# Modulation sums interleaved with the next group's products, and the last pair's normalisation moved into the output projection

## The reference, cut to what matters

```python
mod_lat = jax.nn.silu(c) @ w_mod[l] + b_mod[l]          # 9 x 1024 values, and the same for c_ctx
...
h = _modulate(_rmsnorm(x, norm_g[0]), sh1, sc1)
x = x + 0.5 * g1[:, None, :] * _swiglu(h, ffn_gate[0], ffn_up[0], ffn_down[0])
...
y_sum = ys[0] + ys[1]
mean = jnp.mean(y_sum, axis=-1, keepdims=True)          # over the 64 values of a head
var = jnp.mean(jnp.square(y_sum - mean), axis=-1, keepdims=True)
y_gn = ((y_sum - mean) * lax.rsqrt(var + GN_EPS)).reshape(B, S, D_RWKV) * ln_w + ln_b
gate = jax.nn.sigmoid(gd) @ g2
y_rwkv = (y_gn + (bonuses[0] + bonuses[1]).reshape(B, S, D_RWKV)) * gate
mixed = jnp.concatenate([y_four, y_rwkv], axis=-1).astype(h.dtype)
return mixed @ w_out, finals[0], finals[1]
```

## Time and profile before

| | |
|---|---|
| median of 3 runs | 2886.95 us (2882.22 to 2894.52) |
| the profiled execution | 2874.92 us |
| its span in the trace | 2873.1 us |
| PE busy | 2657.5 us (92%) |
| DVE busy | 1440.4 us (50%) |
| ACT busy | 702.7 us (24%) |
| mean granted TensorE clock | 0.949 of full speed |

### The profile page before, as it was taken

One profiled execution on the slowest core, in us unless ns is written; L12 is line 12 of the kernel. 1 busy time (PEld: TensorE's weight loads), 2 busy tenths in 40 slices (PEclk: granted clock), 3 DMA queues, 4 the chain that ended last, 5 costly groups with the idle time before them and its releaser, 6 DMA issues. The chain is left out here.

```text
span 2873.1 us, 51540 instructions
## 1 busy us (share of the span) xinstructions
PE 2657.5 (92%) x21182; PEld 2522.9 (88%) x21182; DVE 1440.4 (50%) x2749; ACT 702.7 (24%) x1340; POOL 87.7 (3%) x158
## 2 busy tenths in 40 slices
PE   5999999999999799976979797869999999999998
PEld 3999999999999799945868676669999999999998
DVE  4654455555533866317484867433733333433444
ACT  3311111111112411124444454221411111111113
POOL 0000000000000000000111120200000000000000
PEclk8999999999999899987898898989999999999999
DMA  7222222222210222242121212050211111111101
GB/s 277 66 81 75 82 68 80 70 82 82 82 37 1 61 78 93 71 182 53 43 64 40 64 40 64 12 184 27 76 41 41 44 44 44 31 42 44 44 22 67
DMA packets 216144, 193.84 MB, mean 67 GB/s; under 512 B 64787, under 2 KB 184382, under 8 KB 215998
## 3 DMA queue, kind: packets, MB, share of 16 engines
q1 hardware_dynamic: 206512, 166.49, 18.4%
q10 hardware_dynamic: 9486, 25.26, 3.2%
HBM read 159.01 MB, written 32.70 MB: 67 GB/s over the span
## 5 line engine op out<-in xcount | busy, mean ns | idle before, releaser
L129 PE MATMUL ff_ps<-h_hi,ff_wlo 128*128 128x384 f32 x2112 | 712.3, 337 | 7.3 <-DVE h_lo L478 3.7
L131 PE MATMUL ff_ps<-h_hi,ff_whi 128*128 128x384 f32 x2112 | 710.1, 336 | 0.0
L130 PE MATMUL ff_ps<-h_lo,ff_whi 128*128 128x384 f32 x2112 | 709.7, 336 | 0.0
L674 DVE TENSOR_TENSOR ff_s<-ff_ps,ff_s 128x384 f32<-128x384 f32 x132 | 73.6, 557 | 680.6 <-PE ff_ps L131 678.3
L129 PEld LDWEIGHTS ff_ps<-h_hi,ff_wlo 128*128 128x128 f32 x2112 | 400.0, 189 | 10.9 <-DVE h_lo L478 6.7
L130 PEld LDWEIGHTS ff_ps<-h_lo,ff_whi 128*128 128x128 f32 x2112 | 400.3, 190 | 0.0
L131 PEld LDWEIGHTS ff_ps<-h_hi,ff_whi 128*128 128x128 f32 x2112 | 399.6, 189 | 0.0
L129 PE MATMUL ff_ps<-ff_uhi,ff_wlo 128*128 128x384 f32 x1056 | 355.6, 337 | 10.9 <-DVE x L685 10.9
L131 PE MATMUL ff_ps<-ff_uhi,ff_whi 128*128 128x384 f32 x1056 | 353.0, 334 | 0.0
L130 PE MATMUL ff_ps<-ff_ulo,ff_whi 128*128 128x384 f32 x1056 | 352.9, 334 | 0.0
L613 ACT ACTIVATE ff_s<-ff_ps 128x384 f32<-128x384 f32 x132 | 64.9, 491 | 775.8 <-PE ff_ps L131 775.8
(11 more groups left out here) (289 smaller groups left out, 3300.9 us busy)
## 6 DMA issues: line engine op xcount, KB each, us to landing
ff_n<-w_mod ACTq DMA_DIRECT2D x64, 384.0 KB, 3.3
ff_raw<-ffn_w_gate SPq DMA_DIRECT2D x44, 512.0 KB, 4.0
ff_raw<-ffn_w_up SPq DMA_DIRECT2D x44, 512.0 KB, 4.0
ff_raw<-ffn_w_down SPq DMA_DIRECT2D x44, 512.0 KB, 4.5
md_w<-w_mod SPq DMA_DIRECT2D x3, 4096.0 KB, 30.6
pj_raw<-w_in SPq DMA_DIRECT2D x19, 512.0 KB, 4.0
z_dram<-pj_zo SPq DMA_DIRECT2D x15, 576.0 KB, 2.9
rw_rkv<-z_dram SPq DMA_DIRECT2D x12, 576.0 KB, 5.8
```

Source lines behind the costliest of these rows:

```text
L129: pe.matmul(out, w_lo, x_hi, start=start, stop=False)
L130: pe.matmul(out, w_hi, x_lo, start=False, stop=False)
L131: return pe.matmul(out, w_hi, x_hi, start=False, stop=stop)
L674: dve.tensor_tensor(hid[:, t % 2, :], ps[:, 2 + t % 2, 0:CW], silu[:, t % 2, :], ALU.mult)\
```

## The change

Three things are edited.

1. `Modulation.sum` no longer stands at a group's end. Its 12 matmuls are issued one by one in the next group, each behind one k step (three matmuls) of the first gate tile (8 of them) and the first up tile (4). `keep` moves behind the next group's first hidden tile on DVE. Groups 1 and 9 are written out beside the loop.
2. The two slices behind updates 11 and 19 on DVE are each parted by vector: one instruction behind updates 9, 11, 17 and 19.
3. `rw_last` is gone. Its work stands in `output_stage`, among the loads and splits of that stage, and the last row of the mixed input is taken from SBUF (`y`) instead of being stored to DRAM and loaded. Buffers of the RWKV stage that it needs are kept in SBUF until the end of the output stage.

```diff
-        if k:
+        if k or not isinstance(g, int):
             act.wait_ge(self.used, g * (2 * KD) + (2 * k - 2 * KD))
         else:
-            act.wait_ge(self.kept, g)
+            act.wait_ge(self.kept, 1)
...
+    def slice(self, dve, g, k, vectors=(0, 1)):
+        for s in vectors:
+            if s == vectors[0]:
+                dve.wait_ge(self.w_in, g * (16 * KD) + (16 * (k + 1) - 16 * KD))
+                if k:
+                    dve.wait_ge(self.used, g * (2 * KD) + (2 * k - 2 * KD))
...
-    def sum(self, pe, g):
-        pe.wait_ge(self.used, g * (2 * KD))
-        pe.wait_ge(self.kept, g)
-        for j in range(self.COLS // P):
-            for s in range(2):
-                last = pe.matmul(self.ps[:, 2 * j + s:2 * j + s + 1], self.acc[:, s, j * P:(j + 1) * P],
-                                 self.sb["cst"][:, C_ONE:C_ONE + 1], start=True, stop=True)
-        last.then_inc(self.summed, 1)
+    def sum(self, pe, g, n):
+
+        if n >= 2 * self.COLS // P:
+            return
+        if n == 0:
+            pe.wait_ge(self.used, g * (2 * KD) - 2 * KD)
+            pe.wait_ge(self.kept, g - 1)
+        j, s = divmod(n, 2)
+        ins = pe.matmul(self.ps[:, n:n + 1], self.acc[:, s, j * P:(j + 1) * P], self.sb["cst"][:, C_ONE:C_ONE + 1],
+                        start=True, stop=True)
+        if n == 2 * self.COLS // P - 1:
+            ins.then_inc(self.summed, 1)
 
     def keep(self, dve, g):
-        dve.wait_ge(self.summed, g)
+        dve.wait_ge(self.summed, g - 1)
...
+                                if rest and t == 0:
+                                    rest.sum(pe, g, base // 2 * KD + k)
...
                 group(0, True)
                 if rest:
-                    with pe.Fori(1, rest.BLOCKS + 1) as g:
+                    group(1, False)
+                    with pe.Fori(2, rest.BLOCKS + 1) as g:
+                        group(g, False, rest=rest)
+                    group(rest.BLOCKS + 1, False, rest=rest)
+                else:
+                    with pe.Fori(1, GROUPS - 1) as g:
                         group(g, False)
-                        rest.sum(pe, g)
-                with pe.Fori(1 if rest is None else rest.BLOCKS + 1, GROUPS - 1) as g:
-                    group(g, False)
                 group(GROUPS - 1, False, True)
...
-                def group(g, last=False, opening=False, rest=None):
+                def group(g, last=False, opening=False, rest=None, keep=None):
                     for t in range(NC if opening else 0, TILES):
                         hidden(g, t)
+                        if keep and t == 0:
+                            keep.keep(dve, g)
                         if rest:
                             rest.slice(dve, g, t)
...
-                        if n in (11, 19) and rest:
-                            rest.slice(dve, g, TILES + (n == 19))
+                        if n in (9, 11, 17, 19) and rest:
+                            rest.slice(dve, g, TILES + (n > 15), (n // 2 % 2, ))
...
-                    with dve.Fori(1, rest.BLOCKS + 1) as g:
-                        group(g, rest=rest)
-                        rest.keep(dve, g)
+                    group(1, rest=rest)
+                    with dve.Fori(2, rest.BLOCKS + 1) as g:
+                        group(g, rest=rest, keep=rest)
+                    group(rest.BLOCKS + 1, keep=rest)
...
+def output_stage(nc, io, sb, rw, md, xd):
...
+        act_t = Steps(st.sem("act_s"), ["w0", "sq", "w1", "gate", "m0", "sqrt", "m1", "m2", "m3", "m4", "affine", "m5", "m6", "m7"] +
+                      [f"w{o}" for o in range(2, KD)])
+        dve_t = Steps(st.sem("dve_s"), ["y", "centre", "w0", "w1", "var", "m0", "inv", "wide", "m1", "m2", "norm0", "norm1", "m3",
+                                        "norm2", "m4", "bonus", "m5", "gate", "m6", "m7"] +
                       [n for o in range(KD) for n in [f"x{o}_{c}" for c in range(NC)] + [f"w{o + 2}"] * (o + 2 < KD)])
...
-                for k in range(KD):
+                for k in range(LAST):
...
                 upper(0)
+                dve_t.wait(act, "centre")
+                act_t.did("sq", act.activation(c2, y, ACT.Square))
                 upper(1)
-                for k in range(KD):
-                    act.wait_ge(m_in[k % MS], 16 * (k // MS + 1))
-                    act_t.did(f"m{k}", act.activation(m_hi[:, k, :], m[:, k % MS, :], ACT.Copy))
+                pe_t.wait(act, "gate")
+                act_t.did("gate", act.activation(b3(gate), ps[:, 3:6, 0:CW], ACT.Copy))
+                row(0)
+                dve_t.wait(act, "var")
+                act_t.did("sqrt", act.activation(inv, inv, ACT.Sqrt))
+                for k in range(1, 5):
+                    row(k)
+                dve_t.wait(act, "norm2")
+                act_t.did("affine", act.activation(y, y, ACT.Identity, bias=par("ln_b"), scale=par("ln_w")))
+                for k in range(5, KD):
+                    row(k)
                 for o in range(2, KD):
                     upper(o)
...
+                dve_t.wait(pe, "y")
+                over("mean", 0, sb["cst"][:, C_BLK:C_BLK + P], y)
+                over("gate", 3, rw.g2[:, :], rw.lora[:, 2, :])
+                act_t.wait(pe, "sq")
+                pe_t.did("var", head_sums(pe, sb, ps[:, VAR, :], c2))
+                row(0)
+                dve_t.wait(pe, "wide")
+                for c in range(2):
+                    pe_t.did(f"root{c}", spread(pe, sb, ps[:, ROOT[c], :], wide, c))
+                row(1)
+                dve_t.wait(pe, "norm0")
+                pe_t.did("root2", spread(pe, sb, ps[:, ROOT[2], :], wide, 2))
+                for k in range(2, KD):
+                    row(k)
...
+                def norm(c):
+                    pe_t.wait(dve, f"root{c}")
+                    dve_t.did(f"norm{c}", dve.tensor_tensor(y[:, cols3(c)], ps[:, ROOT[c], 0:CW], y[:, cols3(c)], ALU.mult))
+                dve_t.did("y", dve.tensor_tensor(y, y, yb, ALU.add))
+                pe_t.wait(dve, "mean")
+                dve_t.did("centre", dve.scalar_tensor_tensor(b3(y), ps[:, 0:3, 0:CW], -1.0 / HS, b3(y), ALU.mult, ALU.add))
                 lower(0)
                 lower(1)
-                for k in range(KD):
-                    act_t.wait(dve, f"m{k}")
-                    dve_t.did(f"m{k}", dve.tensor_tensor(m_lo[:, k, :], m[:, k % MS, :], m_hi[:, k, :].bitcast(F32), ALU.subtract))
+                pe_t.wait(dve, "var")
+                dve_t.did("var", dve.tensor_scalar(inv, ps[:, VAR, 0:2 * NT], 1.0 / HS, GN_EPS, ALU.mult, ALU.add))
+                row(0)
+                act_t.wait(dve, "sqrt")
+                dve_t.did("inv", dve.reciprocal(inv, inv))
+                dve_t.wait(dve, "inv")
+                dve_t.did("wide", widen(dve, wide, inv))
+                row(1)
+                row(2)
+                norm(0)
+                norm(1)
+                row(3)
+                norm(2)
+                row(4)
+                act_t.wait(dve, "affine")
+                dve_t.did("bonus", dve.tensor_tensor(y, y, rw.bonus[:, :], ALU.add))
+                row(5)
+                act_t.wait(dve, "gate")
+                dve_t.wait(dve, "bonus")
+                dve_t.did("gate", dve.tensor_tensor(y, gate, y, ALU.mult))
+                row(6)
+                row(7)
...
-def rw_last(nc, sb, rw, md, p):
...
-        rw_last(nc, sb, rw, md, NP - 1)
+    return rw
```

More of the change, by code:

```diff
@@ L555, in _, with group @@
             def _(pe):
-                def group(g, first, last_one=False):
+                def group(g, first, last_one=False, rest=None):
                     if first:
@@ L649, in _ @@
                 if rest:
-                    with act.Fori(1, rest.BLOCKS + 1) as g:
+                    group(1, rest=rest)
+                    with act.Fori(2, rest.BLOCKS + 1) as g:
                         group(g, rest=rest)
@@ L1041, in _ @@
                     act_t.did(f"S{j}", act.activation(sine[:, j, :], ps[:, 4 + j, :], ACT.Copy))
-def output_stage(nc, io, sb, md, xd):
-    RAW, MS = 2, 4
-    x = sb["x"]
+def output_stage(nc, io, sb, rw, md, xd):
+    RAW, MS, LAST = 2, 4, KD - 1
+    x, y, yb, wide, c2 = sb["x"], rw.y[:, :], rw.work[:, 2 * T:3 * T], rw.work[:, 0:T], rw.work[:, T:2 * T]
+    gate = rw.work[:, 3 * T:4 * T]
+    b3 = lambda t: t.rearrange("p (c n) -> p c n", c=NC)
+    cols3 = lambda c: slice(c * CW, (c + 1) * CW)
+    inv = rw.mp[:, 0, 0:2 * NT]
+    par = lambda n: rw.pp[:, PP[n]:PP[n] + 1]
     with Stage(nc) as st, nc.psum_tensor("op_ps", [P, 8, 512], F32) as ps, \
@@ L1085, in upper, with row @@
                     act_t.did(f"w{o}", act.activation(w_hi[:, o % 2, :], raw[:, o % 2, :], ACT.Copy))
+                def row(k):
+                    if k < LAST:
+                        act.wait_ge(m_in[k % MS], 16 * (k // MS + 1))
+                    else:
+                        dve_t.wait(act, "gate")
```

(32 more changed lines are left out.)

103 lines of the change are left out of this document (22 added, 81 removed).

## The result

| | before | changed |
|---|---|---|
| first timing: median (lowest to highest, runs) | 2884.59 (2879.56 to 2894.52, 4) | 2842.47 (2836.92 to 2844.58, 4) |
| second timing | 2879.94 (2871.18 to 2889.66, 11) | 2850.08 (2844.31 to 2856.73, 6) |
| profiled execution, span | 2873.1 | 2835.1 |

The ratio is 0.9847 (0.9816 to 0.9878) in the first timing and 0.9888 (0.9866 to 0.9909) in the second. I had 2854 us and a ratio of 0.9886. Faster, as forecast, but by 42 us in the first timing where I had 33; its median lies 11.5 us under my 2854, at the very low end of my range. The second timing, by 30 us, fits.

What follows compares the result with a forecast made beforehand. PE, busy for 92% of the span, was taken as the bound. The terms 0 - 9.5 - 3.4 - 20.1 = -33.0 us, taken from the median 2886.95, gave 2854 us (chance 0.69); range 2842 to 2870 us.

Steps and rivals of the forecast that it cites:

- A1, the pair's price: Modulation's sums on PE, spread as 12 pairs a group: 0.224 us a pair, 2.69 us a group as before, so 0 us.
- R1: Rival, chance 0.11: each pair of spread sums costs a drain, 0.36 us instead of 0.224; +13 us, 2867 us.
- A1, the clock: PE's clock behind the modulation's sums no longer drops once they are spread: six drops of 1.59 us, -9.5 us.
- R2: Rival, chance 0.05: the clock does not hold through the interleaved stretch in groups 2 to 9; 9.2 us a group, 2937 us.
- A2: `keep` moved behind a hidden tile on DVE, and ACT's first load of a group no longer waiting for it: 0 us.
- A3: DVE's parted slices shorten PE's waits for updates in the modulated groups: 0.42 us a group, -3.4 us in eight.
- B: Last pair's normalisation merged into the output stage: first product -21.9 us, 18 passes +2.2, clock -0.4; sum -20.1 us.
- R3: Rival, chance 0.10: the output projection starts early but then waits for `x` or the third weight tile; 5 us, 2859 us.
- R4: Rival, chance 0.05: the merged output stage does not start early, because an overlooked wait chains its first row to the normalisation; 2874 us.
- the last one of the sum: Whole kernel: the profiled 2874.92 us becomes 2841.9; with the same 33.0 us taken from the median 2886.95, 2854 us.

Runs made afterwards that it cites:

- e6: The changed kernel with each one-column sum issued twice in its slot, so four passes behind every three products; periods of 81.68 us.
- e4: The kernel before with only the sums spread, the slices left in pairs; ratio 0.9998 (0.9977 to 1.0018), periods of 79.76 or 79.77 us.
- e5: The changed kernel with the 12 sums as one block again, among products in the next group's first gate tile; five periods of 79.0 us, two of 80.6.
- e2: The kernel before with the output stage's part of the change alone; median 2855.55 us, ratio 0.9938 (0.9917 to 0.9959).
- e3: The kernel before with only the slices parted, the sums still a block at the group's end; ratio 0.9963 (0.9936 to 0.9990).
- e8: The changed kernel with ACT's and DVE's queues reordered in the output stage; first product 11.2 us behind the normalisation's start instead of 12.7, stage 123.00 us.

## Why the prediction was right and where it was off

- **A1, the pair's price: right.** I had 0.224 us; it is 0.226, and e6 shows the same again for four passes. The price of a drain (R1, and the 166 ns that the formula of the Trainium skill, page "TensorE: Matmul & The Clock Gate", section "Single matmul latency", gives for one column) doesn't show: with products on both sides a one-column pass costs 0.113 us.
- **A1, the clock: right**, 9.5 us predicted, 9.1 in e4. R2 fell: the clock stayed at 1.00 even in e6. e5 shows the cause to be the block, not the boundary. My six drops were those of one execution: e2 has the same six (behind groups 1, 2, 3, 5, 6 and 8), but e3 had three and e5 two. What decides which blocks cost their clock is not shown.
- **A2: right.** No wait appeared.
- **A3, mis-sized.** The term was "0.22 us of wait shrinks, with its restart, but doesn't vanish", 0.42 us a group; it vanished, and the term measures 0.71 (e3). I had priced an update in that queue at 0.72 us and a slice at 0.97; they step at 0.66 and 0.92, since in these rows an instruction's recorded duration runs on past the next one's start. That is 2.3 us more over eight groups.
- **B: right in its sum**, -20.1 predicted, -20.4 measured. Its terms: 12.67 us to the first product where I had 13.2 (the four instructions on ACT follow each other without handovers), 2.0 for the 18 passes where I had 2.2. For the clock I had misread: the 4.96 us hold 15 products, not 16, so 2.4 us were lost before. In the profile after, 15 products took 4.93 us, 2.3 lost, and nothing was regained; in the second profile they took 4.21, 1.6 lost, so the term differs from execution to execution. R3 and R4 fell: `x` landed 4.8 us ahead of its reader, where I had 4.
- **The step that failed is the last one of the sum:** "It lies 12 us under the median of the runs shown, 2886.95, and I take the same difference from the median". With it I took everything that the change doesn't touch as constant, the pairs' stage above all, which has no term in my sum. The first median came out 11.5 us under my 2854. Of these, 5.0 are in the profile (38.0 us gained instead of 33.0): 2.5 in the two parts that I had priced, 4.2 in the pairs' stage, 0.5 in the second feed-forward stage, less 2.2 in the other stages. The remaining 6.5 are that difference itself: the changed kernel's profile lies 5.6 us under its median, not 12, and 1.6 in the second timing. My range had no term for this either. Its lower end came from cheaper pairs or slices, and of these only 2.3 us came true, so that the first median lies at its edge and not outside, and the second one near my forecast, is luck.
- **What the runs show in its place:** the pairs' stage took 540.67 to 562.14 us in the profiles without the added matmuls, some 11 us for each scan that loses its clock, and 540.67 and 551.60 for the changed kernel itself. The unprofiled runs show no stages, but each has its mean granted clock on record. Over 39 runs of the kernel before it goes with the time, from 0.952 at 2866.57 us to 0.941 at 2891.40; a straight line through them gives 23 us for 0.01. The two timings of the change have means of 0.953 and 0.950, which is 7 us by that line (an estimate), and their medians lie 7.6 apart. So the difference between 42 and 30 us is one of the clock; that it was lost in the scans is the likeliest reading and not shown.
- **Open:** e4's runs gained nothing in the median while its trace shows 9 us saved. Its profiled execution had three slow scans. Its ten runs had a mean clock of 0.9472 against 0.9462 before, where six drops gone are worth 0.003 alone (9.5 of 2878 us); by the same line some 5 of the missing 9 us are clock lost elsewhere, and the rest is not explained. Nor is it settled whether a kernel's earlier timing makes slow scans likelier.

## What to carry to other kernels

Here small matmuls that stood as a block cost their passes and, behind some of the blocks, the clock of the products that followed; the same passes spread singly among products cost the passes alone. Before a stage is called constant, take its time from several profiles: here one untouched stage moved by 21 us, more than the whole modulation part was worth. Nor does one profile's distance from the median carry over to the next kernel. When work is queued behind a pair of long instructions, step them by the distance of their starts, not by their recorded durations.

## What the runs showed of the hardware that I had not expected

- A scan whose clock falls at its start stays at 1.2 GHz for 27 to 31 us, though PE is recorded as busy for nearly all of it (25.99 of 26 us from 1405 in the profile before); its steps take 3.67 to 4.74 us instead of 2.06 to 2.65. It recovers only in its second half, where steps take 2.1 us whether the scan was slow or not.
- Starting row 0 of the output stage 1.5 us earlier (e8) did not bring the rise of the clock forward: measured from the stage's start it came at 17.2 us, and at 16.1 to 17.6 us in the nine profiles with the later start, so the earlier products all ran slow.
- The fp32 `keep_clock` matmul of 128x256 costs 0.46 to 0.50 us at full clock (3.72 us for eight, 1.99 for four), more than the 0.17 us of an fp32r product of 384 columns.
